# One-hots in two instructions per group, and GpSimd's subtractions tied to them

## The reference, cut to what matters

```python
def peer(h, wq, subkeys, u_tab, v_tab):          # per chunk of 128 tokens
    q = (hc @ wq).reshape(t, 8, 2, 128)
    s = einsum("thpk,pnk->thpn", q, sk)
    s1, i1 = top_k(s[:, :, 0], 16); s2, i2 = top_k(s[:, :, 1], 16)
    best, j = top_k((s1[..., :, None] + s2[..., None, :]).reshape(t, 8, 256), 16)
    e = i1[j // 16] * 128 + i2[j % 16]           # 8 x 16 experts of 16384 for each token
    gate = softmax(best)
    act = gelu(einsum("thkd,td->thk", u_tab[e], hc))
    return einsum("thk,thkd->td", gate * act, v_tab[e])
```

## Time and profile before

| | us |
|---|---|
| median of 3 runs | 3139.86 |
| lowest and highest run | 3136.67, 3146.48 |
| the profiled execution: its own time | 3141.54 |
| its span in the trace | 3139.8 |
| PE busy | 2904.3 (93%) |
| VectorE busy | 2430.9 (77%) |
| POOL busy | 1424.9 (45%) |
| ACT busy | 1207.3 (38%) |

### The profile page before, as it was taken

One profiled execution on the slowest core, in us unless ns is written; L12 is line 12 of the kernel. 1 busy time (PEld: TensorE's weight loads), 2 busy tenths in 40 slices (PEclk: granted clock), 3 DMA queues, 4 the chain that ended last, 5 costly groups with the idle time before them and its releaser, 6 DMA issues.

```text
span 3139.8 us, 50852 instructions
## 1 busy us (share of the span) xinstructions
PE 2904.3 (93%) x15754; PEld 2554.2 (81%) x15754; DVE 2430.9 (77%) x4532; ACT 1207.3 (38%) x1590; POOL 1424.9 (45%) x878
## 2 busy tenths in 40 slices
PE   5888999999998899999899899999999989999997
PEld 3657999989888788888777689989888878888885
DVE  7965679999995688888765307799999937888887
ACT  2333333345553333333333324333555523333332
POOL 2623367776667122222324244777766651222221
PEclk8999999999999999999999899999999989999998
DMA  6336567779898899999935124777788898999996
GB/s 240 134 128 221 199 206 240 242 263 349 308 350 321 301 353 350 355 356 352 351 122 174 66 100 138 229 251 239 277 328 328 310 348 308 352 353 351 357 347 232
DMA packets 352434, 849.74 MB, mean 271 GB/s; under 512 B 30048, under 2 KB 194016, under 8 KB 350176
## 3 DMA queue, kind: packets, MB, share of 16 engines
q1 hardware_dynamic: 239888, 479.53, 44.5%
q0 software_dynamic: 73728, 268.47, 23.6%
q10 hardware_dynamic: 38736, 100.84, 8.1%
HBM read 741.76 MB, written 106.95 MB: 270 GB/s over the span
## 4 chain that ended last, share of the span: by engine, by line
PE 54%; DVE 21%; issue 11%; POOL 7%; DMA 4%; ACT 1%; SPq 0%; POOLq 0%; DVEq 0%; ACTq 0%
PE bank L1418 11%; PE bank L1419 11%; PE bank L1420 11%; POOL w_lo L407 6%; DVE oh_c L995 5%; DVE oh_j L999 5%; PE bank L1360 4%; PE bank L1362 4%; PE bank L1361 4%; DVE rows L1160 2%; PE bank L1260 2%; PE bank L1262 2%; PE bank L1261 2%; DVE oh_i L996 2%; DMA x<-u_rows,u_idx 1%
## 5 line engine op out<-in xcount | busy, mean ns | idle before, releaser
L407 POOL TENSOR_TENSOR w_lo<-w_raw,w_hi 128x1024 fp32r<-128x1024 f32 x338 | 838.6, 2481 | 694.1 <-ACT w_hi L517 692.2
L517 ACT ACTIVATE w_hi<-w_raw 128x1024 fp32r<-128x1024 f32 x594 | 629.1, 1059 | 1346.3 <-PE bank L1420 668.6
L1360 PE MATMUL bank<-h_hi,w_hi 128*128 128x384 f32 x2048 | 702.7, 343 | 42.5 <-POOL w_lo L407 29.8
L1362 PE MATMUL bank<-h_lo,w_hi 128*128 128x384 f32 x2048 | 688.9, 336 | 0.0
L1361 PE MATMUL bank<-h_hi,w_lo 128*128 128x384 f32 x2048 | 688.3, 336 | 0.0
L461 POOL DMA_INDIRECT shared<-stream,v_idx x256 | 246.8, 964 | 830.9 <-DVE rows L1069 746.6
L1418 PE MATMUL bank<-w_hi,h_hi 128*128 128x512 f32 x1536 | 600.7, 391 | 16.6 <-ACT h_hi L642 14.3
L1419 PE MATMUL bank<-w_hi,h_lo 128*128 128x512 f32 x1536 | 600.0, 391 | 0.0
L1420 PE MATMUL bank<-w_lo,h_hi 128*128 128x512 f32 x1536 | 599.8, 390 | 0.0
L1039 DVE TENSOR_TENSOR w_lo<-w_raw,w_hi 128x1024 fp32r<-128x1024 f32 x256 | 313.7, 1226 | 199.9 <-ACT w_hi L517 199.0
L1360 PEld LDWEIGHTS bank<-h_hi,w_hi 128*128 128x128 f32 x2048 | 387.1, 189 | 58.9 <-issue 55.9
(11 more groups left out here) (193 smaller groups left out, 3584.6 us busy)
## 6 DMA issues: line engine op xcount, KB each, us to landing
w_raw<-stream SPq DMA_DIRECT2D x600, 512.0 KB
act_dram<-act_words ACTq DMA_DIRECT2D x256, 192.0 KB
gate_dram<-shared ACTq DMA_DIRECT2D x12, 4096.0 KB, 16.1
act_words<-act_dram SPq DMA_DIRECT2D x256, 192.0 KB
shared<-gate_dram SPq DMA_DIRECT2D x128, 384.0 KB
oh_j<-mod_rows SPq DMA_DIRECT2D x60, 512.0 KB, 4.7
oh_i<-mod_rows SPq DMA_DIRECT2D x20, 512.0 KB, 5.4
shared<-mod_rows SPq DMA_DIRECT2D x16, 512.0 KB, 14.0
```

The source lines that it names most:

```text
L407: nc.gpsimd.tensor_tensor(lo_of(grp, s), w_raw[:, s, :], hi_of(grp, s).bitcast(F32), ALU.subtract).then_inc(S["lo_ready"], 1)
L517: nc.scalar.activation(hi_of(grp, s), w_raw[:, s, :], ACT.Copy).then_inc(S["hi_ready"], 1)
L1360: MM(o, hi, h_hi[:, k, P:T], start=(k == 0), stop=False)
L1362: ins = MM(o, hi, h_lo[:, k, P:T], start=False, stop=(k == KC - 1))
```

## The change

It has six parts.

1. `oh_i` (two buffers) and `oh_c` (one) become one tensor `oh_ic` of three. One comparison writes `oh_c` and the group's `oh_i` together, 2048 elements; one multiplication writes all three parts of `oh_j`, 3072 elements. Five instructions become two.
2. So that one instruction can read them, the keys and the gates are stored by group (`keys_t`, `gate_p`); the copies that fill them write the same elements to other places.
3. `early_dots` runs once in a block, at its end: 18 early dots in a layer in place of 36. The early fetches are 6 in a block in place of 12.
4. `dots_to(g)` is 18 + 2g in place of 36 + g + (g + 1) // 2: two dots in each group.
5. In a group the dots come first, then the one-hots.
6. In the groups 1 to 47 POOL's subtraction for tile 68 + g waits for the semaphore `oh_ready`, until the one-hots of group g - 1 are done.

```diff
-EARLY = 2 * DB * EARLY_SET
+EARLY = DB * EARLY_SET
 def dots_to(g):
-    return EARLY + g + (g + 1) // 2
+    return EARLY + 2 * g
...
                 for g in range(TILES_PER_BLOCK, EXPERT_TILES):
+                    group = g - TB * TILES_PER_BLOCK - RING
+                    if 1 <= group < GROUPS:
+                        pool.wait_ge(S["oh_ready"], l * GROUPS + group)
                     make_lo(first + g // RING, g % RING)
                     b, r = g // TILES_PER_BLOCK, g % TILES_PER_BLOCK
-                    group = g - TB * TILES_PER_BLOCK - RING
                     if b < TB:
-                        end = 2 * (b - 1) * EARLY_SET + min(max(r - 1, 0), EARLY_SET) + (
-                            EARLY_SET if r == TILES_PER_BLOCK - 1 else max(r - 10, 0))
+                        end = (b - 1) * EARLY_SET + min(max(r - 2, 0), EARLY_SET)
                     elif group < GROUPS:
                         end = min(dots_to(max(group - 1, 0)) + U_RING, n + 2)
...
-                    keys = iota_2[:].unsqueeze(1).to_broadcast([P, PAIR, NK, 2])
+                    keys = iota_2[:].unsqueeze(1).to_broadcast([P, 2 * PAIR, NK, 2])
...
-                    V.tensor_tensor(oh_c[:], keys, of_group(j_t, g), ALU.is_equal).then_inc(S["oh_cmp"], 1)
-                    V.tensor_tensor(oh_i[:, s, :, :, :], keys, of_group(i_t, g), ALU.is_equal)
+                    V.tensor_tensor(oh_ic[:, s:3:2 - s, :, :, :], keys, of_group(keys_t, g), ALU.is_equal
+                                    ).then_inc(S["oh_cmp"], 1)
                     dve.wait_ge(S["oh_cmp"], groups + g + 1)
-                    for w in range(3):
-                        ins = V.tensor_tensor(oh_j[:, s, w, :, :, :], oh_c[:], of_group(gate_p[:, w, :], g), ALU.mult)
-                    ins.then_inc(S["oh_ready"], 1)
+                    V.tensor_tensor(oh_j[:, s, :, :, :, :], oh_c.unsqueeze(1).to_broadcast([P, 3, PAIR, NK, 2]),
+                                    of_group(gate_p, g), ALU.mult).then_inc(S["oh_ready"], 1)
...
                 for g in range(GROUPS):
-                    one_hots(g)
                     for n in range(dots_to(g), dots_to(g + 1)):
                         dot(n)
+                    one_hots(g)
```

More of the change, by code:

```diff
@@ L135, in build @@
         PAIR = GROUP // 2
-        oh_i = sb("oh_i", [P, 2, PAIR, NK, 2], BF16)
-        oh_c = sb("oh_c", [P, PAIR, NK, 2], BF16)
+        oh_ic = sb("oh_ic", [P, 3, PAIR, NK, 2], BF16)
+        oh_i, oh_c = oh_ic[:, 0:2, :, :, :], oh_ic[:, 2, :, :, :]
         oh_j = sb("oh_j", [P, 2, 3, PAIR, NK, 2], BF16)
@@ L147, in build @@
         key_words = mix_words[:].bitcast(BF16)
-        gate_p = key_words[:, 0:3 * DT].rearrange("p (a b) -> p a b", a=3)
-        i_t = key_words[:, 3 * DT:4 * DT]
-        j_t = key_words[:, 4 * DT:5 * DT]
+        gate_p = key_words[:, 0:3 * DT].rearrange("p (g w t) -> p g w t", w=3, t=GROUP)
+        keys_t = key_words[:, 3 * DT:5 * DT].rearrange("p (g w t) -> p g w t", w=2, t=GROUP)
         u_more = sb("u_more", [P, U_RING - 4, D])
@@ L174, in build @@
         best_e = topk_part(HEADS, TOPK)
-        cand2 = oh_c[:].rearrange("p a b c -> p (a b c)").bitcast(F32)[:, 0:HEADS * NCAND].rearrange(
+        cand2 = oh_c.rearrange("p a b c -> p (a b c)").bitcast(F32)[:, 0:HEADS * NCAND].rearrange(
             "p (a b) -> p a b", a=HEADS)
@@ L239, in build @@
         mod_b_ring = [oh_words[:, i * D:(i + 1) * D] for i in range(3)]
-        mod_b_ring.append(oh_i[:].rearrange("p a b c d -> p (a b c d)").bitcast(F32))
+        mod_b_ring.append(oh_i.rearrange("p a b c d -> p (a b c d)").bitcast(F32))
         v_row_ring = part(8192, V_RING, D)
@@ L847, in peer_dve, with early_dots @@
                 LINKS = 20
-                def early_dots(b, half):
-                    if isinstance(b, int):
-                        return
+                def early_dots(b):
                     for r in range(EARLY_SET):
-                        had = l * len(range(r, SLOTS, U_RING)) - 2 + half + 1
-                        dve.wait_ge(u_ld[r], b * 32 + 16 * had)
+                        had = l * len(range(r, SLOTS, U_RING))
+                        dve.wait_ge(u_ld[r], b * 16 + 16 * had)
                         V.scalar_tensor_tensor(out=u_row(r), in0=u_row(r), scalar=1.0, in1=rows[:], op0=ALU.mult,
-                                               op1=ALU.mult, accum_out=dots[:, bass.ds(b * 2 * EARLY_SET
-                                                                                       + (half - 2) * EARLY_SET + r, 1)]
+                                               op1=ALU.mult, accum_out=dots[:, bass.ds(b * EARLY_SET + r - EARLY_SET, 1)]
                                                ).then_inc(S["dot"], 1)
@@ L885, in retrieve @@
                     then_top(ins)
-                    early_dots(b, 0)
                     chained(V.tensor_copy(top_f[:], top_i[:]))
@@ L960, in retrieve @@
                     at = (b - 1) * P
-                    V.tensor_copy(i_t[:, bass.ds(at, P)], ps[4][:, 0:P])
-                    V.tensor_copy(j_t[:, bass.ds(at, P)], ps[4][:, P:2 * P])
+                    for w in range(2):
+                        V.tensor_copy(keys_t[:, bass.ds((b - 1) * (P // GROUP), P // GROUP), w, :],
+                                      ps[4][:, w * P:(w + 1) * P].rearrange("p (g t) -> p g t", t=GROUP))
                     chained(V.tensor_copy(gate_t[:, bass.ds(at, P)], ps[4][:, 2 * P:3 * P]))
-                    early_dots(b, 1)
+                    early_dots(b)
                 retrieve(0, 0, True)
@@ L976, in peer_dve @@
                 for part_no in range(3):
-                    link(V.tensor_copy(gate_p[:, part_no, :], gate_t[:]))
+                    left = gate_t[:].rearrange("p (g t) -> p g t", t=GROUP)
+                    link(V.tensor_copy(gate_p[:, :, part_no, :], left))
                     if part_no < 2:
-                        link(V.tensor_tensor(gate_t[:], gate_t[:], gate_p[:, part_no, :], ALU.subtract))
+                        link(V.tensor_tensor(left, left, gate_p[:, :, part_no, :], ALU.subtract))
                 groups = l * GROUPS
                 def of_group(t, g):
-                    return t[:, g * GROUP:(g + 1) * GROUP].rearrange("p (a b) -> p a b", b=2).unsqueeze(2
-                                                                     ).to_broadcast([P, PAIR, NK, 2])
+                    n = t.shape[2]
+                    return t[:, g, :, :].rearrange("p n (a b) -> p (n a) b", b=2).unsqueeze(2
+                                                                   ).to_broadcast([P, n * PAIR, NK, 2])
                 def one_hots(g):
                     s = g % 2
-                    keys = iota_2[:].unsqueeze(1).to_broadcast([P, PAIR, NK, 2])
+                    keys = iota_2[:].unsqueeze(1).to_broadcast([P, 2 * PAIR, NK, 2])
                     if groups + g >= 2:
```

## The result

The changed kernel takes 3283.87 us (median of 3 runs, 3278.97 to 3290.16) against 3139.86: 1.0456 times as long, with a 95% interval of 1.0417 to 1.0496. The forecast was 3296, so its sign and size are right; which part of the change the time goes to is another matter, and the experiments correct that. The profiled execution took 3290.16 us, 148.6 more than the one before.

| stage | before | after | difference |
|---|---|---|---|
| tile 0 to the first one-hot matmuls (block stage) | 314.2, 315.8 | 305.6, 305.6 | -18.8 |
| first to last one-hot matmuls (groups) | 286.7, 292.8 | 372.0, 368.7 | +161.2 |
| last one-hot matmuls to the second half | 70.9, 65.0 | 66.9, 66.6 | -2.3 |
| all the rest | | | +8.5 |

What follows compares the result with a forecast made beforehand. PE bounds most of the span, VectorE the colliding groups by 0.6 us; the new fetch loop would bound the groups. Groups +182, block stage -20, behind the groups -8: +154 on 3141.5, so 3296 us; 8 in 10: 3205 to 3350.

Steps and rivals of the forecast that it cites:

- One-hots: VectorE in each group: the two long instructions take 2.8 us, between 2.7 and 3.2.
- The loop: Groups: wait, subtraction, fetches, dots and one-hots take 14.03 us per two groups, so no group under 7.0 us.
- the landing: Fetches in the groups: 6.0 us from a fetch's issue to the dot that waits for it.
- rival A: Groups: collision was all; fetches land within 3.2 us, PE runs at 5.62 a group, 3062 us; 8% with its twin.
- The gate transfers: ACT's 4 MB transfers between groups delay caught fetches: 11 us each, 5 to 14, five a layer, 55 us.
- Rival B: Groups: the loop holds but a fetch caught by a gate transfer costs 5 us or less; 3215 to 3230; 14%.
- The stage: The 48 groups of a layer take 381 us, against 286.7 and 292.8; 182 us more in all.
- Block stage: Before the groups: PE waits less for `w_lo` and a late gate; 20 us saved, between 8 and 28.
- Behind the groups: After the groups, with 14 dots in place of 20: 8 us saved in all, between -4 and 16.
- The clock (C): Groups: PE's clock stays low from idling, a group takes twice 5.62 us, 3600 us; 4%.
- D: VectorE's one-hots: the long instructions lose their rate, 5.7 us, +136 us, 3430; 4%.
- what is queued behind the wait decides: POOL's queue in the groups: fetches behind the wait serve VectorE two groups later; PE waits about 1.4 us a group.

Runs made afterwards that it cites:

- e5: The changed kernel storing only one of 128 rows of each block of gates, later loads reading the weight stream; 3155.2 us, 1.0028 times the kernel before.
- e1: The changed kernel with POOL's wait for the one-hots taken out; 3238.7 us, 1.0300 times the kernel before.
- e2: The changed kernel with its wait, each fetch let through one group sooner, still behind the subtraction; 3192.6 us, 1.0155 times the kernel before.
- e9: The changed kernel with fetches ahead of POOL's wait and subtraction, let through by the same dots; 3191.1 us, 1.0140 times the kernel before.
- e8: The changed kernel with fetches ahead of wait and subtraction, let through one group sooner than in e9; 3136.4 us, 0.9965 times the kernel before.
- e7: e2 with seven dots per four groups instead of eight; 3159.8 us, 1.0048 times the kernel before.
- e10: e8 with seven dots per four groups instead of eight; 3108.2 us, 0.9882 times the kernel before.
- e12: e8 with three dots per two groups instead of two in each; 3118.6 us, 0.9917 times the kernel before.
- e4: The kernel before, its own dots and no wait, with only the one-hots in two instructions; 3132.2 us, 0.9954 times the kernel before.
- e3: The kernel before with its own dots, plus one-hots in two instructions and POOL's wait; 3119.2 us, 0.9931 times the kernel before.
- e11: e3 with e8's edit: fetches ahead of wait and subtraction, with more lead; 3145.3 us, 1.0000 times the kernel before.

## Why the prediction was right, and where its reason was not

- **One-hots.** Predicted 2.8 us; measured from the start of `oh_ic` to the end of `oh_j` 3.01 (773.54 to 776.55), inside the bounds of 2.7 to 3.2. The 3072 elements took 1.76 where three instructions took 1.93.
- **The loop.** Predicted 14.03 us for two groups, measured 13.34: the reaction 0.08 instead of 0.27, subtraction to fetch 2.53 as said, from the first fetch to the end of the second dot 773.54 - 765.82 = 7.72 against 8.40, one-hots 3.01 against 2.8. The mis-sized term is the landing: the first dot waited 0.18 us for its fetch and began 771.16 - 765.82 = 5.34 us behind the issue, where I took 6.0. I also had the path go through the second fetch, but the second dot followed the first without a wait of its own, so its fetch landed in no more than 772.39 - 767.07 = 5.32 and the 1.26 us between the issues drop out; the path is 5.34 and two dots. I had the 6.0 from the block stage and held the heavier load in the groups for a reason to stay there. The load turned out lighter (276 GB/s against 320); that this made the landing shorter is not shown. With e5 the loop alone is 6.7 us a group, against 7.0. The Trainium skill's figure, "DMA: Bandwidth & Descriptors", Anatomy of one DMA, gives 3.2 us for this transfer; the trace with its 5.34 doesn't agree, and rival A, which rested on such a landing, is refuted.
- **The gate transfers.** Predicted 11 us each (5 to 14), measured 11.5 by e5. Rival B, which needed 5 or less, is out.
- **The stage** came to 372.0 and 368.7 for a predicted 381: the 44 steps of a layer were each 0.3 us too long in the sum, the five transfers each 0.5 too short.
- **Block stage.** Predicted -20, measured -18.8. PE's waits there, with the earlier trace rows, in layer 0 from 480 to 638.7 us and in layer 1 from 2090 to 2287 us:

```profile
PE bank L1361 <- POOL w_lo L407: 1.8, 2, 0.9
```

```profile
PE bank L1361 <- ACT w_hi L519: 3.7, 3, 1.3
PE bank L1361 <- issue: 3.2, 1, 3.2
PE bank L1361 <- POOL w_lo L407: 0.9, 1, 0.9
```

  9.2 became 1.8, and the wait for the gate is gone.
- **Behind the groups.** Predicted -8, measured -2.3 (-3.9 and +1.6), inside its bounds. The longest wait for `w_lo` in layer 0 stayed (5.6, then 5.7 us), so I was wrong to expect it to shrink with fewer dots. What shrank there is the wait at the start of the second half, from 9.6 to 3.9 us.
- **The clock (C).** 0.93 in the stage where it was 1.00. Behind PE's wait of 10.69 us the 24 one-hot matmuls took 2.74 us, behind 2.32 us 1.55: it fell at the transfer steps, and there is no steady fall. That a short fall is hidden was not quite right. Between 728 and 738 us, in the wait of 10.69 us and just behind it, the granted clock was 0.50, the lower of its two levels. From 738 to 745 us PE was busy without a gap at a mean of 0.87, and the step there took 7.89 us. In layer 0 PE is busy 9.4 us longer than in e5 (285.4 against 276.0), so by my estimate up to 1.9 of a transfer's 11.5 us are the clock's. D needed one-hots of 5.7 us and is out.
- **The step that was wrong** is the sentence that what is queued behind the wait decides, with all of the stage's loss put down to that. The arithmetic was right with all parts in place, and its split was near: 72 us for the loop and 110 for the transfers, measured by e5 as 45.8 and 115.4. But I never worked it out without the wait. e1 does: 112.7 of the 161.2 us are there without it, nearly all at the transfers, and the wait adds 48.5, which is about the loop's share. So the wait lengthens the loop, but the transfers' share doesn't come from it. It comes from the short lead of the fetches, and this is shown: let through one group sooner and then two, with the wait and the dots unchanged, they bring the steps over a transfer from 12.4 to 18.6 us (after) to 12.6 to 13.4 (e2, e9) and 6.5 to 7.6 (e8), and with seven dots in four groups from 8.8 to 11.4 (e7) to none to be seen (e10).
- **What stays argued** is why the lead got short. Two dots a group empty the ring of six buffers in three groups instead of four. That fewer dots help is shown with lead added (e2 to e7, e8 to e10 and e12), but e1 differs from e4 in three things at once: fewer early dots, two in a group, and dots ahead of the one-hots. No run takes that order alone. That the wait harms in part by what is queued behind it is shown by its cost, 48.5 us with the fetches behind it and 17.8 with them ahead. That with the dots as before the same wait gains time, e3 against e4 makes likely and doesn't show.

## What to carry to other kernels

A wait put ahead of one instruction is a wait for everything queued behind it on that engine: issue the transfers first, then wait (e2 and e9, the same order: 93 to 95 us given back by it alone). But a fetch put first must not itself wait for something later in the other engine's order (e11). And before pricing a change of several parts as one loop, work the loop out with each part alone: here what was there without the wait, the dots' new schedule, cost twice what the wait did.

## What the runs showed of the hardware

- **A POOL issue of an indirect transfer is lengthened beside VectorE's long one-hots**: 1.76 to 1.82 and 1.47 us in place of 0.95 and 0.94 (e2, e8). In the kernel before, beside five short ones, one took 1.22. I had priced the issue at 0.95, and it turned POOL's queue of some 5 us into one of 6.1 to 6.2, the bound of the ordinary steps of e2 and e8.
- **The subtraction and the one-hots block each other by who starts first**: `oh_ic` takes 2.12 us if a subtraction of 2.40 began 1.37 us before it, 3.26 if it began 0.24 us before it (e10), and 1.22 with none. The Trainium skill says so in "SBUF — State Buffer", Who interferes with whom: an instruction of VectorE with two inputs in SBUF contends with one of GpSimd that reads it, and the one issued first has its way; the trace agrees. The dots, with one input in PSUM, kept 1.21 to 1.22 us beside the same subtraction.
- **A 4 MB transfer holds the fetches issued around it**: in e8 the fetch issued at 713.66 was read by the dot at 731.25, 17.6 us later; in the changed kernel's loop it is 5.3. How long the step over it gets depends on how early the fetches were let through: 15.7 us in e1, 13.1 in e9, 7.3 in e8, no longer than its neighbours in e10.
